# One layer of a decoder trunk: wide transposes in an inverse, state products left out, projection halves loaded apart

## What is computed

```python
def _rwkv_step(state, inp):
    r_t, w_t, k_t, v_t, a_t, b_t = inp
    sa = jnp.einsum('bhvk,bhk->bhv', state, a_t)
    state = (state * w_t[:, :, None, :] + sa[..., None] * b_t[:, :, None, :]
             + v_t[..., None] * k_t[:, :, None, :])
    y = jnp.einsum('bhvk,bhk->bhv', state, r_t)
    return state, y
...
merged = jax.nn.sigmoid(ga) * (y_a @ proj_a[l]) + jax.nn.sigmoid(gb) * (y_b @ proj_b[l])
x = x + merged @ w_out[l]
```

## Time and profile before

| What | Value |
|---|---|
| median of 3 runs | 703.69 us (703.23 to 704.12) |
| the profiled execution | 706.06 us |
| its span | 704.2 us |
| PE busy | 663.6 us (94%) |
| DVE busy | 436.1 us (62%) |
| ACT busy | 294.6 us (42%) |
| mean granted clock of PE | 0.971 of full |

### The profile page before, as it was taken

How to read it: one execution, slowest core, us unless ns; L and a number is a source line. 1 busy time by engine, 2 the same in 40 slices (tenths; PEclk the granted TensorE clock), 3 DMA queues, 4 the chain that set the end, 5 groups by cost and what they waited for, 6 DMA issues and landing times.

```text
span 704.2 us, 16194 instructions
## 1 busy us (share of the span) xinstructions
PE 663.6 (94%) x7036; PEld 635.8 (90%) x7036; DVE 436.1 (62%) x483; ACT 294.6 (42%) x330; POOL 96.5 (14%) x72
## 2 busy tenths in 40 slices
PE   6999999999988899999999987969899999999996
PEld 6999999999988788977888886969899999999996
DVE  4866666656668965737865333756866566666552
ACT  5544444444342335423545442434444444443331
POOL 1100000001137634000004421101400000000110
PEclk9999999999999989989999999989999999999999
DMA  7756555456557353313131212145455565655451
GB/s 245 217 171 194 189 181 179 164 192 198 164 187 206 125 180 121 121 60 119 61 121 63 64 63 63 30 151 161 150 168 179 180 181 187 195 172 188 165 164 60
DMA packets 100402, 105.28 MB, mean 149 GB/s; under 512 B 2028, under 2 KB 98532, under 8 KB 100356
## 3 DMA queue, kind: packets, MB, share of 16 engines
q1 hardware_dynamic: 99492, 101.77, 45.3%
q0 software_dynamic: 848, 2.83, 1.4%
q10 hardware_dynamic: 16, 0.00, 0.0%
HBM read 103.53 MB, written 1.06 MB: 149 GB/s over the span
## 4 chain that ended last, share of the span: by engine, by line
PE 82%; DVE 12%; issue 3%; ACT 2%; DMA 1%; DVEq 0%; SPq 0%; ACTq 0%
PE two L1299 23%; PE two L1300 21%; PE two L1301 21%; PE two L1295 10%; DVE w_lo L817 3%; PE two L1425 2%; DVE h_m L823 1%; DVE gates L1017 1%; DVE hlo_f L841 1%; DMA w_raw<-in_proj_b 1%; DVE h_f L823 1%; DVE w_lo L833 1%; PE two L1526 1%; PE two L1527 1%; PE two L1528 1%
## 5 line engine op out<-in xcount | busy, mean ns | idle before, releaser
L502 ACT ACTIVATE w_hi<-w_raw 128x2048 fp32r<-128x2048 f32 (+1 forms) x88 | 166.1, 1888 | 285.3 <-PE two L1301 261.6
L817 DVE TENSOR_TENSOR w_lo<-w_raw,w_hi 128x2048 fp32r<-128x2048 f32 (+1 forms) x88 | 202.3, 2299 | 86.0 <-ACT w_hi L502 85.9
L1299 PE MATMUL two<-hlo_f,w_hi 128*128 128x256 f32 x704 | 200.1, 284 | 4.7 <-DVE w_lo L833 2.5
L1301 PE MATMUL two<-hhi_f,w_hi 128*128 128x256 f32 x704 | 198.8, 282 | 0.0
L1300 PE MATMUL two<-hhi_f,w_lo 128*128 128x256 f32 x704 | 198.8, 282 | 0.0
L1299 PEld LDWEIGHTS two<-hlo_f,w_hi 128*128 128x128 f32 x704 | 133.8, 190 | 6.6 <-DVE hlo_f L841 4.6
L1300 PEld LDWEIGHTS two<-hhi_f,w_lo 128*128 128x128 f32 x704 | 133.7, 190 | 0.1
L1301 PEld LDWEIGHTS two<-hhi_f,w_hi 128*128 128x128 f32 x704 | 133.7, 190 | 0.0
L1299 PE MATMUL two<-hid_lo_t,w_hi 128*128 128x256 f32 x352 | 99.4, 282 | 0.5
L1300 PE MATMUL two<-hid_hi_t,w_lo 128*128 128x256 f32 x352 | 98.9, 281 | 0.0
L1301 PE MATMUL two<-hid_hi_t,w_hi 128*128 128x256 f32 x352 | 98.8, 281 | 0.0
(11 more groups left out here) (303 smaller groups left out, 952.6 us busy)
## 6 DMA issues: line engine op xcount, KB each, us to landing
w_raw<-in_ffn_up SPq DMA_DIRECT2D x22, 1024.0 KB, 5.3
w_raw<-in_ffn_gate SPq DMA_DIRECT2D x21, 1024.0 KB, 5.3
w_raw<-in_w_in SPq DMA_DIRECT2D x20, 1024.0 KB, 5.1
w_raw<-in_ffn_down SPq DMA_DIRECT2D x16, 896.0 KB, 4.7
w_raw<-in_ffn_down SPq DMA_DIRECT2D x8, 1024.0 KB, 5.2
w_raw<-in_w_out SPq DMA_DIRECT2D x4, 1024.0 KB, 5.1
w_raw<-in_proj_a SPq DMA_DIRECT2D x4, 512.0 KB, 3.8
w_raw<-in_proj_b SPq DMA_DIRECT2D x4, 512.0 KB, 5.4
```

Source lines behind the costliest of these rows:

```text
L502: nc.scalar.activation(whi[slot][:, 0:kts], raw[slot][:, 0:kts], ACT.Copy).then_inc(sg["hi_ready"], 1)
L817: nc.vector.tensor_tensor(wlo[slot][:, 0:kts], raw[slot][:, 0:kts], whi[slot][:, 0:kts].bitcast(F32), ALU.subtract).then_inc(sg["lo_ready" ...
L1299: mm(dst, whi[slot][:, k_, cols], xl, start=start, stop=False)
L1301: return mm(dst, whi[slot][:, k_, cols], xh, start=False, stop=stop)
```

## The change

- *Two-block transposes.* `TT` is laid out so that the two blocks of a head lie side by side. In levels 1 to 4 one transpose of 64 by 128 takes the place of two products with the identity; level 0 keeps them. All transposes of a level now run first and all `U` products behind them, each with one signal for the end.
- *Unread products left out.* Chunk 3's cells of `by_token` for `bct` and `kct`, `phi` of chunks 0 and 3, `psi` of chunk 3 and `rh` of chunk 0 are not made. `dpc` and `phi` hold two chunks.
- *One product instead of two in `y_state`.* DVE adds `AR` to `rh` in `read_add` when it takes it from PSUM; ACT copied it before.
- *Gate pieces.* In the levels 23 behind `U` and 13 behind the level's product (20 and 16 before); then 4 behind `x1`, 3 behind `asa`, 3 behind `asx`, 2 each behind `phi`, `psi` and `rh`, none between the output steps.
- *Projection halves.* The upper half has semaphores of its own (`pa_in0`, `pa_in1`). For chunks 2 and 3 it is loaded once the difference of the half in its buffer is made (`pa_lo`), the lower half on `lo_ready` as before. `late_hi(N_PROJ + 1, ...)` comes ahead of the norm for both halves, POOL makes both differences, and ACT's half of chunk 2 stands between the two halves of the norm's result.

The diff, cut:

```diff
-            dpc = one[:, :, 0:C].rearrange("p (j J r) n -> p r J j n", J=2, r=2)
-            phi = run[:].rearrange("p a b -> p (a b)")[:, 0:1024].rearrange("p (r J j n) -> p r J j n", r=2, J=2, j=HT)
+            dpc = one[:].rearrange("p a b -> p (a b)")[:, 0:512].rearrange("p (r j n) -> p r j n", r=2, j=HT)
+            phi = run[:].rearrange("p a b -> p (a b)")[:, 0:512].rearrange("p (r j n) -> p r j n", r=2, j=HT)
...
-                TT = vv[:].rearrange("p j t -> p (j t)").rearrange("p (s J j t) -> p s J j t", s=2, J=2, j=HT)
+                TT = vv[:].rearrange("p j t -> p (j t)").rearrange("p (J j s t) -> p s J j t", s=2, J=2, j=HT)
+                TTs = vv[:].rearrange("p j t -> p (j t)").rearrange("p (J j a) -> p J j a", J=2, j=HT)
...
-                    with sp.Fori(0, D // W // 2) as i:
-                        for s in range(2):
-                            cols = bass.ds(i * (2 * W) + s * W, W)
-
-                            sp.wait_ge(sg["lo_ready"], 2 * i + N_PROJ + s - 1)
-                            sp.dma_start(raw[s][:, 0:HT], proj_w[0][:, :, cols]).then_inc(w_landed[s], 16)
-                            sp.dma_start(raw[s][:, HT:2 * HT], proj_w[1][:, :, cols]).then_inc(w_landed[s], 16)
+                    for c in range(D // W):
+                        s, cols = c % 2, slice(c * W, (c + 1) * W)
+                        if c < 2:
+                            sp.wait_ge(sg["lo_ready"], N_PROJ + c - 1)
+                        else:
+                            sp.wait_ge(sg["pa_lo"], c - 1)
+                        sp.dma_start(raw[s][:, 0:HT], proj_w[0][:, :, cols]).then_inc(sg[f"pa_in{s}"], 16)
+                        if c >= 2:
+                            sp.wait_ge(sg["lo_ready"], N_PROJ + c - 1)
+                        sp.dma_start(raw[s][:, HT:2 * HT], proj_w[1][:, :, cols]).then_inc(w_landed[s], 16)
...
-            pool.wait_ge(sg["late_hi"], 3)
-            nc.gpsimd.tensor_tensor(wlo[0][:, 0:4], raw[0][:, 0:4], whi[0][:, 0:4].bitcast(F32), ALU.subtract)\
-                .then_inc(sg["pa_lo"], 1)
-            pool.wait_ge(sg["hi_ready"], N_PROJ + 1)
-            nc.gpsimd.tensor_tensor(wlo[0][:, 4:KD], raw[0][:, 4:KD], whi[0][:, 4:KD].bitcast(F32), ALU.subtract)\
-                .then_inc(sg["lo_ready"], 1)
-            pool.wait_ge(sg["late_hi"], 4)
-            nc.gpsimd.tensor_tensor(wlo[1][:, 0:4], raw[1][:, 0:4], whi[1][:, 0:4].bitcast(F32), ALU.subtract)\
-                .then_inc(sg["pa_lo"], 1)
+            for c in range(2):
+                pool.wait_ge(sg["late_hi"], 3 + c)
+                nc.gpsimd.tensor_tensor(wlo[c][:, 0:4], raw[c][:, 0:4], whi[c][:, 0:4].bitcast(F32), ALU.subtract)\
+                    .then_inc(sg["pa_lo"], 1)
+                pool.wait_ge(sg["hi_ready"], N_PROJ + c + 1)
+                nc.gpsimd.tensor_tensor(wlo[c][:, 4:KD], raw[c][:, 4:KD], whi[c][:, 4:KD].bitcast(F32), ALU.subtract)\
+                    .then_inc(sg["lo_ready"], 1)
...
+                if n >= N_PROJ and half == 0:
+                    act.wait_ge(sg[f"pa_in{n % 2}"], 16)
+                else:
+                    act.wait_ge(w_landed[n % 2], 16 * landings(n))
...
-                for i, c in enumerate((1, 0)):
-                    act.wait_ge(sg["t_done"], 2 * lev + i + 1)
+                act.wait_ge(sg["t_done"], lev + 1)
+                for c in range(2):
...
-                    late_hi(N_RKV + 19, 1)
+                    gate_sigmoid(3)
...
-                    gate_sigmoid(3)
+                    late_hi(N_RKV + 19, 1)
             act.wait_ge(sg["x1_done"], 1)
             nc.scalar.activation(X1[:, 1], pairs(1), ACT.Copy).then_inc(sg["x1_ready_act"], 1)
...
-            act.wait_ge(sg["rh_done"], 1)
-            for r_ in range(2):
-                nc.scalar.activation(rhf[:, r_], pairs(4 + r_), ACT.Copy).then_inc(sg["rh_ready"], 1)
             nc.scalar.activation(gs[:, 0, 0:2], cst[:, C_EPS:C_EPS + 2], ACT.Sqrt)
+            late_hi(N_PROJ + 1, 0)
+            late_hi(N_PROJ + 1, 1)
             norm_square(0)
-            late_hi(N_PROJ + 1, 0)
...
-            late_hi(N_PROJ + 1, 1)
-            gate_sigmoid(6)
-            gate_sigmoid(7)
...
-                    act.wait_ge(w_landed[c % 2], 16 * landings(N_PROJ + c))
+                    act.wait_ge(sg[f"pa_in{c % 2}"], 32)
                     act.wait_ge(sg["proj_a"], c - 1)
                 else:
+                    act.wait_ge(w_landed[c % 2], 16 * landings(N_PROJ + c))
...
+            normed_hi(0)
             hi_half(2, 0)
+            normed_hi(1)
+            gate_sigmoid(6)
+            gate_sigmoid(7)
             hi_half(3, 0)
...
+                dve.wait_ge(sg["u_done"], lev + 1)
                 for c in range(2):
-                    dve.wait_ge(sg["u_done"], 2 * lev + c + 1)
...
-                nc.vector.tensor_tensor(phi[:, r_], pairs(r_), dpc[:, r_], ALU.add).then_inc(sg["phi_ready"], 1)
+                nc.vector.tensor_tensor(phi[:, r_], bank[r_][:, 0:HT * C].rearrange("p (j n) -> p j n", n=C), dpc[:, r_],
+                                        ALU.add).then_inc(sg["phi_ready"], 1)
...
-            take(18)
+            dve.wait_ge(sg["rh_done"], 1)
+
+            def read_add(J, c):
+
+                for par in range(2):
+                    hs, x_ = slice(64 * par, 64 * par + 64), c ^ par
+                    own = AR[hs, 1, :, (2 * J + c) * C:(2 * J + c + 1) * C]
+                    nc.vector.tensor_tensor(rhf[hs, x_, J], pairs(4 + x_)[hs, J], own, ALU.add)\
+                        .then_inc(sg["rh_ready"], 1)
...
+            read_add(0, 1)
             state_step(1)
+            read_add(1, 0)
+            read_add(1, 1)
             state_step(2)
+            take(18)
             norm_gain(0)
...
-            dve.wait_ge(sg["lo_ready"], N_PROJ + 1)
-            dve.wait_ge(sg["pa_lo"], 2)
-            lo_half(1, 1)
             gated_a(0)
             gated_a(1)
+            dve.wait_ge(sg["lo_ready"], N_PROJ + 2)
...
+                    if k_ >= 2 and 2 * J + c == NCH - 1:
+                        continue
...
-            def level(lev, c_):
-
-                for J, j, par, c, cols in cells():
-                    old = c ^ par if lev else par
-                    if c == c_:
-                        u = part(spot(c, c ^ par, J, j), NA[halves(c), par, J, j], TT[halves(c), old, J, j], J + j == 0)
-                    else:
-                        t = part(spot(2 + c, c ^ par, J, j), TT[halves(c), old, J, j], cst[halves(c), C_SUI:C_SUI + C],
-                                 J + j == 0)
-                u.then_inc(sg["u_done"], 1)
-                t.then_inc(sg["t_done"], 1)
-
             for lev in range(5):
                 if lev == 0:
-                    pe.wait_ge(sg["n_ready"], 2)
                     pe.wait_ge(sg["tt_eye"], 2)
                     pe.wait_ge(sg["kk_raw"], 4)
+                    for J, j, par, c, cols in cells():
+                        last = part(spot(2 + c, c ^ par, J, j), TT[halves(c), par, J, j], cst[halves(c), C_SUI:C_SUI + C],
+                                    J + j == 0)
+                    pe.wait_ge(sg["n_ready"], 2)
                 else:
                     pe.wait_ge(sg["x_ready"], lev)
                     pe.wait_ge(sg["x_ready_act"], lev)
-                level(lev, 0)
-                level(lev, 1)
-                gate_part(4)
+                    for J in range(2):
+                        for j in range(HT):
+                            for c in range(2):
+                                at = (J * HT + j) * C
+                                last = nc.tensor.transpose(bank[2 + c][:, at:at + C], TTs[halves(c), J, j],
+                                                           cst[halves(c), C_SUI:C_SUI + C])
+                last.then_inc(sg["t_done"], 1)
+                for J, j, par, c, cols in cells():
+                    last = part(spot(c, c ^ par, J, j), NA[halves(c), par, J, j], TT[halves(c), c ^ par if lev else par, J, j],
+                                J + j == 0)
+                last.then_inc(sg["u_done"], 1)
+                gate_part(4 if lev in (0, 4) else 5)
                 if lev == 0:
                     pe.wait_ge(sg["nr_raw"], 2)
                 pe.wait_ge(sg["iu_ready"], 2 * lev + 2)
@@ -1678,7 +1692,7 @@
                     last = part(spot(4 + x_, c, J, j), lhs, rhs, J + j == 0)
                 last.then_inc(sg["x_done"], 1)
                 if lev < 4:
-                    gate_part(4)
+                    gate_part(3 if lev else 4)
 
             pe.wait_ge(sg["kk_ready"], 2)
             for J, j, par, c, cols in cells():
@@ -1691,6 +1705,7 @@
             for J, j, par, c, cols in cells():
                 last = part(spot(2 + c, c ^ par, J, j), G[halves(c), c ^ par, J, j], AX[halves(c), par, J, j], J + j == 0)
             last.then_inc(sg["asa_done"], 1)
+            gate_part(3)
...
+                if 2 * J + c in (1, 2):
```

(27 more changed lines are left out.)

29 lines of the change are left out of this document (13 added, 16 removed).

## The result

The changed kernel takes 681.8 us (median of 4, 679.07 to 684.88) against 703.46 us (median of 4) beside it: a ratio of 0.970 (95% interval 0.965 to 0.976), 21.7 us less. Two more comparisons gave 0.972 (0.968 to 0.975) and 0.973 (0.969 to 0.977), so 18 to 22 us in all. The forecast was 688.3 us with a range of 684 to 695: the sign was right, the gain was larger by 3 to 6 us. One execution of after (1598.91 us, beside e10, whose median without it is 681.20) and one of before (1056.63 us, beside e13) were disturbed; the ratios leave them out.

The account below looks back on a forecast made before the run. TensorE, busy in 94% of the span, was taken as the bound, with gaps from late instructions and a wait for mg. 3.5 + 0.8 - 0.4 + 4.0 + 0 + 7.5 = 15.4 us off 703.69 gave 688.3, range 684.0 to 695.0.

Parts of the forecast that it names:

- instruction stalls with the low clock: Inverse to projections: TensorE's waits for instructions and low clock fall from 9.4 to 5.4 us; gain 4.0, between 0 and 7.
- products left out, their work: In phi, psi and rh 40 products fewer, 1.2 us; three output steps at half, 1.8 us.
- transposes: Levels 1 to 4: 64 wide transposes at 0.04 us replace 128 small products; gain 0.8 us, between -3.9 and +1.6.
- two more groups of gate pieces: Behind asa, phi, psi and rh: each added group costs about 0.2 us at its ends, 0.4 us lost.
- state and outputs: Around the state steps: DVE's added AR additions are set against gate work moved out of the way; 0 us.
- projection halves: Projections: the wait for mg shrinks from 5.5 to 0.5 us and the clock stays up; gain 7.5 us.
- the play: Inverse to projections: blocks every 3.5 us, 2.5 more beside a transfer; 4 to 9 us of stalls left against 11.
- Rival 1: Inverse to projections: instruction stalls stay, as a late block costs the same anywhere; 4.0 us less gain, 692.3 us; chance 0.15.
- rival 3: Levels 1 to 4: wide transposes cost 0.115 us each; 4.7 us less gain, 693.0 us; chance 0.07.
- rival 4: Level 1 to first state product: transposes let the clock fall to 0.5; slower, about 723 us; chance 0.03.
- Rival 2: Projections: the wait for mg is only replaced, by chunk 3's half; term 2.5 instead of 7.5, 693.3 us; chance 0.10.
- Rival 5: Levels and y steps: transposes were already hidden, y steps latency-bound; 2.5 us less gain, 690.8 us; chance 0.10.

Follow-up runs that it names:

- e10: The changed kernel run once more as it is, beside the kernel before: median 682.71 us, 681.20 without the disturbed execution.
- e13: The changed kernel with the left-out products put back into phi, psi, rh and the output steps: 684.17 us, ratio to before 0.974.
- e14: The kernel before, unchanged, profiled a second time: 702.57 us.
- e1: The changed kernel with levels 1 to 4 transposing again by 32 small products instead of 16 wide transposes: 684.51 us, ratio to before 0.976.
- e9: The changed kernel with the projection part undone and ACT's first-half conversion waiting for both halves to land: 690.36 us, ratio to before 0.984.
- e12: The changed kernel with w_out's first chunk taking k_ 0 to 5 of both halves ahead of 6 and 7: 685.03 us.
- e6: The kernel before with the load of projection chunk 2 held until the second state product is done: 697.38 us against 699.93.
- e7: The kernel before with only the nine gate pieces moved from the output steps to behind asa, phi, psi and rh: 696.71 us against 699.93.
- e2: The changed kernel with the nine gate pieces moved back to the output steps: 686.23 us, ratio to before 0.978.
- e3: The changed kernel with the projection part undone, but ACT's first half still waiting for its own semaphore: 685.76 us.
- e4: The kernel before with only the new levels (wide transposes, T ahead of U, gate pieces 5 and 3): 697.11 us against 700.81.

## Why the prediction was off

Forecast and measured, in the stretch of the table (the forecast had 14.9 us there, and 0.5 for the tokens' transposes ahead of it, which no run isolated):

| Term | Forecast | Measured | From |
|---|---|---|---|
| instruction stalls with the low clock | 4.0 | 8.0 to 9.4 | "issue" 8.3 or 7.1 before, 0.6 to 0.8 after; low clock 1.7 in both (0.64 for 4.70 us; 0.66 for 5.03, e14) |
| products left out, their work | 3.0 | 1.6 | e13, 2.9 less 1.3 of stalls |
| transposes | 0.8 | 1.8 | e1, 4.0 less 2.2 of stalls |
| two more groups of gate pieces | -0.4 | not isolated | |
| state and outputs | 0 | 0.3 | waits for `gx` 1.0, less the wait of 0.7 for `read_add` |
| projection halves | 7.5 | 6.7 to 8.6 | e9; before's last column is 7.9 and 8.6 above after's |
| sum | 14.9 | 18.4 to 21.7 | table: 20.4 |

With each trace of before taken by itself the terms add to 20.9 and 20.4. The low clock behind the gap of 3.38 us, and in the second trace behind that of 2.84:

```profile
431.80:436.50 4.70, 4.70 (x124) 4.63 (x125) 1.67 (x4) 0.22 (x1) 0.00 (x0) 0.64 0.02 3
```

**The step that failed** is the stall term: "Playing the new order through block by block ... leaves 4 to 9 us of stalls", of which it took 5.4. Three traces show 0.6 to 0.8 (up to 1.3 in e12). The kind of stall was right: gaps stand at the same instructions in both traces of before, 256 or a multiple of it apart, and e1, e6, e7 and e13 each move them as it says. Wrong was the play, which let blocks come one in 3.5 us, and 2.5 us later beside each transfer, whatever PE did. In the traces a block's transfer starts only once PE has entered the block ahead: mostly 0.5 to 1.3 us behind that border with no load in flight, up to 3.4 us with one, and PE, where it has to wait, goes on 2.2 to 3.3 us after the start. (Borders are counted in steps of 256 records from the gaps.)

So what counts is how long PE takes for the 256 instructions beside each fetch. A level of 6.4 us had 432 matmul and load records, 256 in 3.8 us; it now has 336 in 6.05, 256 in 4.6. From `x1` to the state there were some 940 in 11.96 us, 256 in 3.2 with the gaps counted and 2.9 without; now some 830 in 15.10, 256 in 4.6. A fetch of 3 to 4 us fits into that. Even the one that a load held up fitted: in after PE crosses a border at about 390.3, the transfer starts 2.5 us later, at 392.77, behind the loads issued at 388.45 and 388.88, and PE needs the block only at 395.41. In before a delay of 3.4 us, from 425.97 to 429.36, met dense products that were used up by 428.4. The other loads of after hold a block up by less than 2 us. What stalls is the block of `x1`, whose 256 instructions take 2.4 us. I had averaged the whole stretch (35 us of fetching against 43 of work) and seen 8 us of slack, and then trusted the play over it.

A reading of the prediction is wrong too: in the earlier trace rows the slices of 5 to 10 GB/s are not the block, but four packets of 1 KB of the load's queue. The block's transfer starts at 429.36, inside the slice of 410, as the megabyte's last packets start. That it comes only behind the megabyte stands.

**Right, and mis-sized.** Transposes start 0.04 us apart as forecast, and the clock stays at 1.00; but going back to the small ones costs 1.8 us of work (e1) instead of 0.8. The projection halves: the wait for `mg` is gone and the clock behind it full, 6.7 us in e9 for 7.5. The products left out: 1.6 us of work for 3.0; that e13 comes to 2.9 is luck, since 1.3 of it are stalls. `mg` doesn't wait for chunk 3, whose first half was issued at 424.45, 14 us ahead of its conversion on ACT at 438.82.

**Right by luck.** Moving the gate pieces was costed at -0.4 plus a share of the stalls. Alone it gave 6.6 us (e7; 3.2 by the medians), and taking it back cost 8.2 (e2; 3.5 to 4.6 by the medians). The separate trials on after (4.0, 8.2, 7.2 and 2.9) add to 22.3, more than the 20.4 of the whole; e2's wait of 3.4 us was in neither kernel.

**The rivals.** Rival 1 (stalls stay) and rival 3 (dear transposes) are refuted by three traces, rival 4 by the clock. Rival 2 is half right in mechanism: e3 shows that the wait for `mg` would still be 3.1 us if only the semaphore had been split. Rival 5 is refuted for the transposes by e1 (1.8 us of work) and half right for the products: 1.4 of their 3.0 us weren't there (e13). What it forecast, a smaller gain, didn't come because the stall term was so much larger. The forecast bounded the stall term at a gain of 7; both estimates are above it.

**The median.** It started from 703.69, a median of three; the kernel before then gave 699.9 to 701.2 on four chips. That shifts both kernels' times, not the difference.

## What to carry to other kernels

Where small products run dense, count instructions as well as time: here the levels were free of gaps once 256 TensorE instructions lasted 4.6 us, and gaps came at 3.8 or less, more so with a weight transfer in flight. Slow products that have to run anyway (here 128 by 128 by 256 gate pieces) are best spread among the dense ones, and the buffer that their last one frees sets when the next conversion may stand ahead of latency-bound work on its engine. Price a change at stalls block by block: from where PE enters the block ahead to where it needs the next, against the time that a fetch takes.

## What the hardware showed beyond the forecast

- A second or third trace of the same program repeats the mixing block to 0.3 us while the gaps within it differ by up to 1 us, and whole executions by 6 us and more with the granted clock (0.971 to 0.984 in two traces of before).
- A DVE copy of 128 by 512 within SBUF took 2.17 us beside a POOL operation and 0.43 without, 1.30 and 0.67 when they overlapped in part (e7, e2). In the eight traces where they overlapped it ended 0.28 to 0.29 us behind POOL's operation, whenever it began. By the Trainium skill, page "Trainium Architecture — The Big Picture", section "What this means for kernel authors", DVE and GpSimd share a pair of SBUF ports that one of them holds for itself, which is no split of bandwidth. The traces agree: the copy's end follows POOL's, and isn't stretched in proportion.
- PE's clock fell to 0.5 for some us behind idle gaps of 2.6 to 5.8 us in this block (3.38 and 2.84 in the two traces of before, 2.55 in e4, 3.4 in e2, 4.6 in e9), and stayed at 1.00 behind 2.2 us (e1) and 1.47 (e6). But the length of the gap doesn't settle it. Every trace has a wait of 3.1 to 3.5 us for DVE's `w_lo` at about 245: behind it the clock is 0.50 for 5 us in eleven traces, both first ones among them, and 1.00 in five (e2, e3, e9, e12, e14). Behind one of 1.75 us at about 325 it falls in seven traces of sixteen. So a low clock in a single trace need not be in the other executions; what decides it, no run here shows.
